# Moving the weight ring by 64 bytes in SBUF, in a two-block hybrid layer on one core

## What is computed

```python
# block one
h = rms_norm(x, mix_norm)
parts = split(h @ w_in)                        # 2048 -> 12040: mixer inputs and three gates
y_a, y_b, y_c = s5_mixer(...), hgrn2_mixer(...), mlstm_mixer(...)
merged = sigmoid(g_a) * (y_a @ wb[:512]) + sigmoid(g_b) * (y_b @ wb[512:1280]) \
       + sigmoid(g_c) * (y_c @ wb[1280:])
x = x + merged @ w_out
x = x + conv_ffn(rms_norm(x, ffn_norm), ...)   # 2048 -> 2*5632, conv, silu(a)*b, 5632 -> 2048
x = rms_norm(x, final_norm)
# block two
proj = rms_norm(x, g_mix) @ w_in_2             # latent and dilated attention inputs, two gates
x = x + (g0 * (o_a @ w_o_mla) + g1 * (o_b @ w_o_dil)) @ w_o
gt, up = split(rms_norm(x, g_ffn) @ w_gate_up) # 2048 -> 2*5632
return x + (silu(gt) * up) @ w_down
```

## Time and profile before

| | us |
|---|---|
| median of 3 runs (3098.19 to 3101.96) | 3098.6 |
| the profiled execution | 3111.46 |
| its span, first to last instruction | 3109.7 |
| PE busy with matmuls | 3073.6 |
| DVE busy | 1807.1 |
| ACT busy | 1203.0 |

### The profile page before, as it was taken

One profiled execution on the slowest core, in us unless ns is written; L12 is line 12 of the kernel. 1 busy time (PEld: TensorE's weight loads), 2 busy tenths in 40 slices (PEclk: granted clock), 3 DMA queues, 4 the chain that ended last, 5 costly groups with the idle time before them and its releaser, 6 DMA issues.

```text
span 3109.7 us, 47133 instructions
## 1 busy us (share of the span) xinstructions
PE 3073.6 (99%) x18712; PEld 2737.1 (88%) x18712; DVE 1807.1 (58%) x2356; ACT 1203.0 (39%) x1351; POOL 113.4 (4%) x80
## 2 busy tenths in 40 slices
PE   8999999999999999999999999999999999999999
PEld 8898898889998888888889977788999888888888
DVE  6673352867678888875555333322566666665444
ACT  5443102114444444444443312244445444444333
POOL 0000000000001100000000310000000000000000
PEclk9999999999999999999999999899999999999999
DMA  6554333445555555555555543223455555555555
GB/s 222 188 189 155 109 109 109 157 152 185 183 187 192 196 191 190 197 174 187 189 194 178 186 163 109 81 95 122 163 189 182 197 189 191 197 191 173 187 187 181
DMA packets 80147, 530.23 MB, mean 171 GB/s; under 512 B 9152, under 2 KB 9536, under 8 KB 27712
## 3 DMA queue, kind: packets, MB, share of 16 engines
q1 hardware_dynamic: 80064, 529.07, 49.7%
HBM read 526.94 MB, written 2.10 MB: 170 GB/s over the span
## 4 chain that ended last, share of the span: by engine, by line
PE 97%; DVE 1%; ACT 1%; issue 0%; DMA 0%; SPq 0%; ACTq 0%; DVEq 0%
PE bank L488 97%; DVE w_low L1461 0%; ACT w_high L1031 0%; DVE arena L1461 0%; PE bank L965 0%; DVE arena L1458 0%; DMA xT<-in_xT 0%; DVE arena L1491 0%; DVE xrs L1491 0%; DVE acts_both L1461 0%; DVE xtmp L1461 0%; ACT arena L1116 0%; ACT mix_high L1135 0%; DVE xT L1461 0%; ACT L1154 0%
## 5 line engine op out<-in xcount | busy, mean ns | idle before, releaser
L1461 DVE TENSOR_TENSOR w_low<-ring,w_high 128x2048 fp32r<-128x2048 f32 (+1 forms) x440 | 922.7, 2098 | 438.8 <-ACT w_high L1031 434.8
L1031 ACT ACTIVATE w_high<-ring 128x2048 fp32r<-128x2048 f32 (+1 forms) x448 | 787.4, 1759 | 472.4 <-DMA ring<-in_w_down 235.9
L488 PE MATMUL bank<-hT,ring 128*128 128x256 f32 x2560 | 569.2, 383 | 1.2 <-ACT arena L1378 1.2
L488 PEld LDWEIGHTS bank<-hT,ring 128*128 128x128 f32 x2560 | 488.1, 192 | 75.6 <-issue 7.3
L488 PE MATMUL bank<-acts_both,w_high 128*128 128x512 f32 x1408 | 492.9, 395 | 1.7 <-DVE arena L1461 1.3
L488 PE MATMUL bank<-up_early,w_high 128*128 128x512 f32 x1408 | 488.0, 389 | 1.3 <-issue 0.8
L488 PE MATMUL bank<-up_late,w_high 128*128 128x512 f32 x1408 | 487.3, 389 | 0.0
L488 PE MATMUL bank<-acts_both,w_low 128*128 128x256 f32 x1408 | 394.8, 280 | 0.0
L488 PE MATMUL bank<-up_early,w_low 128*128 128x256 f32 x1408 | 388.6, 276 | 0.0
L488 PE MATMUL bank<-up_late,w_low 128*128 128x256 f32 x1408 | 388.6, 276 | 0.0
L488 PEld LDWEIGHTS bank<-acts_both,w_high 128*128 128x128 f32 x1408 | 264.7, 188 | 63.1 <-issue 1.6
(11 more groups left out here) (277 smaller groups left out, 4084.8 us busy)
## 6 DMA issues: line engine op xcount, KB each, us to landing
ring<-in_w_up SPq DMA_DIRECT2D x176, 1024.0 KB, 4.8
ring<-in_w_down SPq DMA_DIRECT2D x128, 704.0 KB, 4.0
ring<-in_w_in SPq DMA_DIRECT2D x66, 1024.0 KB, 4.8
ring<-in_w_mix SPq DMA_DIRECT2D x62, 1024.0 KB, 4.8
ring<-in_w_gates SPq DMA_DIRECT2D x48, 1024.0 KB, 4.9
ring<-in_w_branch SPq DMA_DIRECT2D x16, 1024.0 KB, 4.8
ring<-in_w_out SPq DMA_DIRECT2D x16, 1024.0 KB, 4.8
ring<-in_w_o SPq DMA_DIRECT2D x16, 1024.0 KB, 4.8
```

The source lines that it names most:

```text
L488: return nc.tensor.matmul(o, lhsT, rhs, start=first, stop=last)
L1031: A(w_high[:, s, 0:cols], ring[:, s, 0:cols], ACT.Copy).then_inc(rounded[s], 1)
L1461: return V.tensor_tensor(o, a, b, op)
```

## The change

Two unused tensors of 64 bytes per partition are allocated: one ahead of the ring, one between the ring and `xT`.

```diff
+        sb("ring_pad", [P, 16])
         ring = sb("ring", [P, RING, UNIT])
         ring_base = nc.sbuf_base - RING * UNIT * 4
+        sb("x_pad", [P, 16])
         xT = sb("xT", [P, KT, T])
```

## The result

The changed kernel takes 3152.65 us (median of 4 runs, 3145.28 to 3156.25), the kernel before 3100.28 us (4 runs, 3098.19 to 3108.65). The ratio is 1.0146, 95% interval 1.0118 to 1.0173: slower by 52 us, where 3068 and at most 3120 had been forecast. In a second round it took 3154.83 us, ratio 1.0149, interval 1.010 to 1.0199.

What follows compares the result with a forecast made beforehand. PE was taken as the bound; savings of 18.0 us (up-projections), 11.8 (down-projections), 0 (three-pass), 0.5 (tokens) and 0 summed to 30.3 us, from median 3098.6 to 3068 us. Range: 3045 to 3120, 8 in 10.

Steps and rivals of the forecast that it cites:

- What bounds the kernel: Whole kernel: PE busy 3073.6 of 3109.7 us, so an address edit pays or costs only through the spacing of matmuls.
- Which operand is loaded meanwhile: Up-projection: 13.2 ns excess beside the low load, 6.8 beside the high; same start modulo 128 as the moving tile costs more.
- Two signs against its own reading: Excess nearly even per column (0.442 and 0.443 ns) in the up-projection, and the flat three-pass stage; both cited for "no change".
- no change: Rival: excess goes by columns, from moving reads or result writes, so weight alignment is nothing; 3099 us, chance 0.29.
- The other sign: Three-pass projections: starts 120, 110 and 130 ns apart, the matmul beside the low load shortest, so no dearer low load.
- Three-pass stages 0: Three-pass projections, 1984 low loads: no gain taken; bound about 20 us if the low load's excess vanished.
- plain fp32 0: Plain fp32 matmuls, some 2800 records: three offsets show one price, so 0, with 3 us as the bound.
- tokens -0.5 us: Token projections, where weights move: 3 ns in favour of the 64-byte offset on 160 matmuls, 0.5 us saved.
- DVE, ACT and DMA 0: Engines and DMAs using the ring 64 bytes on: no cost taken; DVE would have to grow 17% to bind the up-projection.
- The activations' move modulo 256 worth 0: Activations going from 128 to 0 modulo 256: no row prices it, taken as 0.
- The slower rival: A load 64 bytes off costs 6 ns more on 6208 low loads: 37 us, 3136 us, chance 0.28.
- The page against the rows: Skill page's independent TensorE read ports would make a start address free, change worth 0 not 30 us; trace shows 13.2 ns.

Runs made afterwards that it cites:

- the first profile of before: The kernel before the change, unchanged, in its first profiled execution: span 3109.7 us, both down-projections at 350 ns per step.
- before once more: The unchanged kernel before, profiled again in another execution: span 3102.5 us, both down-projections at 340 ns per step.
- aligned: The kernel before with W_SHIFT = 0, so both weight tiles and the activations start at 0 modulo 128: 3145.57 us, ratio 1.013.
- the grid: Probe outside the layer: up-projection matmuls alone, high and low weights each 0 to 448 bytes from the moving tile, both orders; no placement below 340.0 ns.
- (192, 0): Distances in bytes of high and low weights from the moving tile, modulo 256, as in the kernel before: 3100.28 us.
- (192, 128): High and low weights' distances in bytes from the moving tile; the kernel before with its ring moved 128 bytes against the rest: 3131.48 us, ratio 1.010.

## Why the prediction was wrong

*What bounds the kernel*, and that only the distance between matmuls can pay or cost, was right: 43.3 us of PE make the 43.1 us of the span.

*The step that failed is "Which operand is loaded meanwhile".* It put 13.2 ns of excess down to the low load and 6.8 to the high one, and took the first to fall to the second. The runs show that the excess doesn't belong to a load. A stage runs in a repeating pattern, and the distances of both loads from the moving tile together limit which periods it can have. In the trace to the nanosecond the 512-column matmul of the up-projection, beside the low load, went from 226.5 to 233.7 ns from start to start; the 256-column one, beside the high load, whose distance didn't change at all, went from 113.5 to 119.6. In place of -6.4 ns a step the up-projections got +13.3 on 2816 steps, +37.5 us for -18.0. The down-projections got +3.3 on 1408 against the first profile of before, +13.3 against the second, for -8.4. Their 19.2 and 10.8 ns were no property of the operands either: the same kernel had them at 13.2 and 6.8 in another execution.

*Two signs against its own reading* were named in the prediction. One was right to follow: 226.5 and 113.5 ns divide the excess evenly by columns, so the load beside a matmul need not be its cause. The rival made "no change" of it, though, and no law follows from it: in the changed kernel the parts are 20.4 and 12.9 ns, no longer as two to one. The other sign was read from four starts at 10 ns, and the reading doesn't hold. Over the 512 steps of block one's and block two's output projections in the trace of before, the matmul beside the low load takes 117.3 ns, between 115.2 and 120.8 for the other two; in before once more the three are 117.8, 117.6 and 117.9. The step is 353.3 ns in both.

*Three-pass stages 0, plain fp32 0, tokens -0.5 us, DVE, ACT and DMA 0*: right in size. The three-pass stages did have periods other than 353.3 to go to (360.0 aligned, 346.7 with the ring moved by 128), so that the 0 was in part luck: the reason given for it was the reading of the earlier trace rows. The token matmuls sum to 700 ns for three in place of 703, which is -0.5 us on 160, but the saving isn't where it was expected: all three kinds now take 396. Landings of the down-projection take 4.0 us as in the earlier trace rows:

```profile
ring<-in_w_down SPq DMA_DIRECT2D x128, 704.0 KB, 4.0
```

*The activations' move modulo 256 worth 0*: right as such (everything moved by 128 is the same). But 256 is the period in which distances count, and the prediction thought in 128. It said it would be wrong altogether if offsets modulo 256 or the relation of the two weights mattered. Both do; for this change it is the relation, as the grid shows.

*The slower rival* had the sign right, with a chance of 0.28, and gave 37 us and 3136; its range ended at 3145. That the up-projections alone lost 37.5 is a coincidence. The rival charged each load at 64 with 6 ns, 17 us in the up-projections and 12 in the three-pass stages, which lost nothing; and the aligned kernel, without any such load, ran those at their slowest. It also set its threshold too low: at the 6 us that the prediction takes as the bound of a measurement, 6208 loads decide from 1 ns each, not from 0.3.

*The page against the rows.* By the rule of the Trainium skill, "SBUF — State Buffer", section "Who interferes with whom", TensorE's two read ports are independent; that a start address is therefore free was the prediction's inference and is not in that section. The measured 1.0146 for an address change speaks against the inference for fp32r matmuls. For plain fp32 the trace agrees with it: `hT,ring`, whose weights did move against the activations, takes 383 ns before and 384 after, and 216 from start to start in both. Whether the ports themselves are what the loads and the moving tile meet at, no run here shows.

*Left open*: what in the chip makes these patterns, and which of its possible periods a stage falls into behind an interruption, 340.0 or 350.0 at (192, 0), 346.7 or 353.3 at (192, 128). No run here tells.

## What to carry to other kernels

If a kernel is bound by TensorE and a change moves a buffer that feeds it, check the distance of its matmuls from start to start before and after, even if no instruction changes: here 64 bytes were 1.5%. Don't put an excess down to the one operand that happens to be read beside it; measure the placements in a small probe, in both orders. Take a mean over many steps before you call one matmul of three the shortest. And profile the kernel before twice, and look at each stage from one interruption to the next: its period in one execution may not be that of the next.

## What the runs showed of the hardware

- fp32r matmuls with a fresh 128-column weight load each ran, at a granted clock of 1.00, in repeating patterns with a period of mostly 340.0, 346.7, 350.0, 353.3 or 360.0 ns per 768 columns in the layer (348.8 once), 6.3 to 12.5% above one column per cycle at 2.4 GHz. Plain fp32 took 216 ns per record against 213.3 in all nine profiles of the layer, with the weight ring at distance 0, 128 and 192.
- In those nine profiles the period changed only where the stream was interrupted (steps over 400 ns apart) and otherwise stayed, for up to 1413 steps.
- The period depends on the distances of both weight tiles from the moving tile, repeating every 256 bytes up to the 448 that were tried, not on their places, and partly on what ran before. Two matmuls of 256 columns with both weights at distance 0 took 240.0 ns together, at distance 64 226.7.
- At the lower granted clock nothing of this is seen: where the clock stood at 1.2 GHz in the trace of before, fp32r matmuls of 256 columns took 213 to 214 ns from start to start, one column per cycle.
